# A two-block transformer kernel: high parts of the weights by converting DMA, six slots, first inputs reordered

## The reference

```
proj = nx @ w_in;  h = h + mixed @ w_out
h = h + square(relu(nm @ w_ff1)) @ w_ff2
... second layer: w_in_2, w_branch, w_out_2 ...
h = h + (silu(nm @ w_ffn_gate) * (nm @ w_ffn_up)) @ w_ffn_down
```

## Time and profile before

| | us |
|---|---|
| median of 3 runs | 1414.1 (1411.76 to 1415.14) |
| the profiled execution | 1414.06 |
| its span in the trace | 1412.4 |
| PE busy in it | 1386.7 (98%) |
| ScalarE busy | 865.4 (61%) |
| VectorE busy | 624.8 (44%) |
| POOL busy | 192.7 (14%) |

### The profile page before, as it was taken

How to read it: one execution, slowest core, us unless ns; L and a number is a source line. 1 busy time by engine, 2 the same in 40 slices (tenths; PEclk the granted TensorE clock), 3 DMA queues, 4 the chain that set the end, 5 groups by cost and what they waited for, 6 DMA issues and landing times.

```text
span 1412.4 us, 17525 instructions
## 1 busy us (share of the span) xinstructions
PE 1386.7 (98%) x6784; PEld 1119.7 (79%) x6784; DVE 624.8 (44%) x1216; ACT 865.4 (61%) x1272; POOL 192.7 (14%) x227
## 2 busy tenths in 40 slices
PE   9999999999999999999989999999999999999999
PEld 6977966788888888887867768787788888888887
DVE  6055365521211212357578779954534422341232
ACT  5574566654544535666678778776557645663561
POOL 0210000111111111111100001011111111111110
PEclk9999999999999999999999999999999999999999
DMA  7975544698888888877745556679988888888975
GB/s 227 248 167 131 143 117 97 151 208 194 189 196 196 194 189 199 189 166 170 169 100 119 120 119 163 169 172 269 221 198 186 192 192 200 192 192 194 197 164 125
DMA packets 72791, 248.00 MB, mean 176 GB/s; under 512 B 8098, under 2 KB 8114, under 8 KB 72580
## 3 DMA queue, kind: packets, MB, share of 16 engines
q0 software_dynamic: 31536, 113.54, 47.0%
q1 hardware_dynamic: 40452, 131.73, 28.9%
q10 hardware_dynamic: 720, 1.61, 0.3%
HBM read 240.52 MB, written 6.32 MB: 175 GB/s over the span
## 4 chain that ended last, share of the span: by engine, by line
PE 78%; ACT 8%; DVE 8%; issue 3%; DMA 2%; SPq 0%; DVEq 0%; ACTq 0%
PE bank L466 24%; PE bank L470 24%; PE bank L473 24%; ACT WH L770 2%; ACT WL L778 1%; PE bank L581 1%; PE bank L600 1%; DVE eb L1416 1%; DMA RAW<-in_w_out 1%; PE bank L624 1%; PE bank L614 1%; ACT eb L924 1%; ACT hs L720 1%; DMA gates<-hs 1%; DVE eb L1412 0%
## 5 line engine op out<-in xcount | busy, mean ns | idle before, releaser
L466 PE MATMUL bank<-NH,WH 128*128 128x512 f32 x1152 | 466.4, 406 | 3.5 <-ACT NH L875 1.7
L470 PE MATMUL bank<-NL,WH 128*128 128x512 f32 x1152 | 449.2, 391 | 1.0 <-DVE NL L1160 0.5
L473 PE MATMUL bank<-NH,WL 128*128 128x512 f32 x1152 | 449.3, 391 | 0.0
L770 ACT ACTIVATE WH<-RAW 128x1024 fp32r<-128x1024 f32 (+2 forms) x227 | 235.2, 1037 | 204.8 <-PE bank L473 191.5
L466 PEld LDWEIGHTS bank<-NH,WH 128*128 128x128 f32 x1152 | 216.9, 188 | 69.0 <-issue 26.3
L470 PEld LDWEIGHTS bank<-NL,WH 128*128 128x128 f32 x1152 | 217.0, 188 | 47.8 <-issue 3.8
L473 PEld LDWEIGHTS bank<-NH,WL 128*128 128x128 f32 x1152 | 216.8, 188 | 46.2
L778 ACT ACTIVATE WL<-WH 128x1024 fp32r<-128x1024 f32 (+2 forms) x219 | 229.5, 1048 | 5.6
L470 PE MATMUL bank<-AL,WH 128*128 128x512 f32 x432 | 168.2, 389 | 0.0
L466 PE MATMUL bank<-AH,WH 128*128 128x512 f32 x432 | 168.1, 389 | 0.0
L473 PE MATMUL bank<-AH,WL 128*128 128x512 f32 x432 | 168.0, 389 | 0.0
(11 more groups left out here) (288 smaller groups left out, 1637.7 us busy)
## 6 DMA issues: line engine op xcount, KB each, us to landing
RAW<-in_w_in SPq DMA_DIRECT2D x64, 512.0 KB, 5.5
RAW<-in_w_ff SPq DMA_DIRECT2D x64, 512.0 KB, 6.2
WL<-in_w_ff POOLq DMA_DIRECT2D x64, 512.0 KB, 8.7
WL<-in_w_in POOLq DMA_DIRECT2D x62, 512.0 KB, 7.8
RAW<-in_w_gu SPq DMA_DIRECT2D x44, 512.0 KB, 6.6
WL<-in_w_gu POOLq DMA_DIRECT2D x44, 512.0 KB, 8.8
RAW<-in_w_down SPq DMA_DIRECT2D x20, 512.0 KB, 5.1
WL<-in_w_down POOLq DMA_DIRECT2D x20, 512.0 KB, 8.7
```

The source lines that it names most:

```text
L466: e.matmul(o, a[0], a[1], start=(k == 0), stop=False)
L470: e.matmul(o, b[0], b[1], start=False, stop=False)
L473: mm = e.matmul(o, c[0], c[1], start=False, stop=(k == t.kt - 1))
L770: e.activation(WH[p % HL][:, 0:n], RAW[p % RAWS][:, 0:n], ACT.Copy).then_inc(*act.sig("high", p))
```

## The change

It does these things:

- From the tenth piece on (`ADDED` = 9), the high part no longer comes over RAW and a ScalarE copy. POOL issues a DMA from the fp32 weights straight into WH, whose type is fp32r, so the transfer converts (`highs`). It is issued at `split_time(p)`, after the product that last used the slot. The negation stands 8.5 after it, the accumulating transfer for WL 10 after it.
- `HL` is 6 instead of 5. RAW moves to memory that the gates' temporaries use later.
- The first unit is cut into pieces of 1, 1, 2, 2, 2 blocks (128 KB each for the first two), so there are 228 pieces.
- The first four blocks of x come in halves of 64 partitions: the lower over SP, the upper over ScalarE's queue.
- VectorE makes NH and NL of block 0 before the low part of the first piece. PE runs two more matmuls of 128 columns on zeros.

```diff
-HL = 5
+HL = 6
...
-            n = 2 if u == 0 else n
-            for k in range(0, kt, n):
-                self.pieces.append((u, k, min(n, kt - k)))
+            at = [0, 1, 2, 4, 6, 8] if u == 0 else [*range(0, kt, n), kt]
+            self.pieces += [(u, a, b - a) for a, b in zip(at, at[1:])]
...
-        RAW = [sb(f"RAW{i}", PIECE) for i in range(RAWS)]
...
+        RAW = [sb(f"RAW{i}", PIECE) for i in range(RAWS)]
+        top[0] = temps
         gx_, gb_, gt_ = two("gX", 5), two("gB", 4), two("gT")
...
-        ADDED = 8
+        ADDED, NEGATED = 9, 8.5
...
+        def high(p):
+            return ("high" if p < ADDED else f"high_loaded{p % HL}", p)
...
-            if p < 5:
-                return [-20.0, -18.4, -15.4, -13.4, -11.5][p]
-            return plan.used[p - HL] + 0.1
+            if p < HL:
+                return [-20.0, -18.4, -17.4, -15.4, -13.4, -11.5][p]
+            return (4.1, 8.1, 12.1)[p - HL] if p < ADDED else plan.used[p - HL] + 0.1
 
         def low_time(p):
-            return split_time(p) + (3.0 if p >= ADDED else 0.05)
+            return split_time(p) + (NEGATED + 1.5 if p >= ADDED else 0.05)
...
-                for n in (S, S, UC):
+                for n in (S, S, UC, P, P):
...
-                        pe.wait_ge(("high", p), hi(x, k0 + k))
+                        pe.wait_ge(high(p), hi(x, k0 + k))
...
-                e.dma_start(first_in, A["xT"][:, 0:64 + S]).then_inc(*act.sig("x0", by=16))
-                at["gains",] = at["x0",]
-                for i in range(2, 8, 2):
+                e.dma_start(first_in[64:P, :], A["xT"][64:P, 0:64 + S]).then_inc(*act.sig("x_upper0", by=16))
+                for i in range(1, 4):
+                    e.dma_start(hT[64:P, i, :], x_src[64:P, i, :]).then_inc(*act.sig(f"x_upper{i}", by=16))
+                for i in range(4, 8, 2):
                     e.dma_start(hT[:, i, :], x_src[:, i, :]).then_inc(*act.sig(f"x{i}", by=16))
...
             def splits():
-                for p, (u, k, m) in enumerate(plan.pieces):
+                for p, (u, k, m) in enumerate(plan.pieces[:ADDED]):
...
                     if p >= ADDED:
-                        yield split_time(p) + 1.5
+                        yield split_time(p) + NEGATED
...
-                yield -19.0
-                dve.wait_ge(("x0",))
+                yield -20.5
+                dve.wait_ge(*x_in(0))
...
-                    yield -18.9 + k
-                    row("attn", "n_attn", k, g_attn, [(f"x{k}",), ("gains",)])
+                    yield -18.9 + k if k else -20.4
+                    row("attn", "n_attn", k, g_attn, x_in(k))
...
+            def highs():
+                for p, (u, k, m) in enumerate(plan.pieces):
+                    if p < ADDED:
+                        continue
+                    yield split_time(p)
+                    st, name, i, kt, cols, k0 = plan.units[u]
+                    src = A[name] if i is None else A[name][i]
+                    u0, j0, m0 = plan.pieces[p - HL]
+                    pool.wait_ge(("product", "block", u0, j0 + m0 - 1))
+                    e.dma_start(WH[p % HL][:, 0:m * cols], src[:, k * cols:(k + m) * cols]).then_inc(
+                        *pool.sig(f"high_loaded{p % HL}", p, by=16))
...
-            yield from merge(zeros(), lows(), masks())
+            yield from merge(zeros(), highs(), lows(), masks())
...
-                for p, (u, k, m) in enumerate(plan.pieces):
+                for p, (u, k, m) in enumerate(plan.pieces[:ADDED]):
                     yield -29.0 + 2 * p if p < RAWS else split_time(p - RAWS) + 0.1
...
-                for i in range(1, 8, 2):
-                    yield -28.5 + i
+                yield -28.0
+                e.dma_start(first_in[0:64, :], A["xT"][0:64, 0:64 + S]).then_inc(*sp.sig("x_lower0", by=16))
+                for i in (1, 2, 3):
+                    yield (-26.0, -24.0, -23.5)[i - 1]
+                    e.dma_start(hT[0:64, i, :], x_src[0:64, i, :]).then_inc(*sp.sig(f"x_lower{i}", by=16))
+                for i in (5, 7):
+                    yield -23.0
                     e.dma_start(hT[:, i, :], x_src[:, i, :]).then_inc(*sp.sig(f"x{i}", by=16))
```

More of the change, by code:

```diff
@@ L333, in build_program, with x_in @@
                 operands[st] = (NH, NL, "n_attn" if st in ("qG", "kG", "vG", "gG", "qD", "kD", "vD") else "n_second")
+        def x_in(k):
+            return [(f"x_lower{k}",), (f"x_upper{k}",)] if k < 4 else [(f"x{k}",)]
         on_act = {"vG", "vD", "vS", "vH"}
-        ADDED = 8
+        ADDED, NEGATED = 9, 8.5
         def freed(t):
@@ L749, in prologue @@
                         e.dma_start(cf, A["c_f32"]).then_inc(*act.sig("const", by=16))
-                    act.wait_ge((f"x{k}",), ("gains",))
+                    act.wait_ge(*x_in(0), *x_in(k))
                     e.activation(NH[:, k, :], hT[:, k, :], ACT.Copy, scale=g_attn[:, k:k + 1]).then_inc(*act.sig(*hi("n_attn", k)))
@@ L754, in prologue @@
                     square("attn", k, acc if k == 0 else sq[k % 2], 1.0,
-                           [(f"x{k}",)] + ([("square_sum", "attn", k - 2)] if k > 2 else []))
+                           x_in(k) + ([("square_sum", "attn", k - 2)] if k > 2 else []))
             def square(ph, k, to, scale, waits):
@@ L774, in negated @@
                     if p >= ADDED:
-                        yield split_time(p) + 1.5
+                        yield split_time(p) + NEGATED
                         n = m * plan.units[u][4]
-                        act.wait_ge(("high", p))
+                        act.wait_ge(high(p))
                         e.activation(WL[p % HL][:, 0:n], WH[p % HL][:, 0:n].bitcast(F32), ACT.Copy,
@@ L826, in gla @@
                 yield gla_time(c, 0) + 0.1
-                act.wait_ge(("gla_gate", c), ("gains",))
+                act.wait_ge(("gla_gate", c), *x_in(0))
                 if c:
@@ L1462, in gain_product @@
                 yield plan.start(("f2", 3))
-                dve.wait_ge(("gains",), lo(("f1", 0), 0))
+                dve.wait_ge(*x_in(0), lo(("f1", 0), 0))
                 e.tensor_tensor(g_fn, g_fin, g_n1, ALU.mult).then_inc(*dve.sig("gain_product"))
@@ L1469, in lower_bound @@
                 yield plan.start("qS") + 1.0
-                dve.wait_ge(("gains",))
+                dve.wait_ge(*x_in(0))
                 e.tensor_tensor(m_, la, lb2, ALU.max).then_inc(*dve.sig("lb", 0))
@@ L1715, in vector @@
             streams += [mixed_split("mixed", k, T_A1 - 2.0 + 0.2 * k, []) for k in range(4)]
-            streams += [dilated(), to_h("wo0", "wo0", lambda k: (f"x{k}",))]
+            streams += [dilated(), to_h("wo0", "wo0", lambda k: x_in(k)[-1])]
             streams += [mixed_split("mixed", k, plan.start("wo1") - 0.6 + 0.1 * k, []) for k in range(4, 8)]
@@ L1783, in weights @@
                     if p >= RAWS:
-                        sp.wait_ge(low(p - RAWS) if p - RAWS < ADDED else ("high", p - RAWS))
+                        sp.wait_ge(low(p - RAWS))
                     e.dma_start(RAW[p % RAWS][:, 0:m * cols], src[:, k * cols:(k + m) * cols]).then_inc(
```

## The result

The changed kernel takes 1493.95 us (median of 4 runs, 1489.64 to 1496.07) against 1414.62 of the kernel before in the same session: ratio 1.0559, 95% interval 1.053 to 1.0589. It is slower by 79 us, and outside the forecast range of 1394 to 1413.

The account below looks back on a forecast made before the run. PE itself was taken as the bound, except in stick-breaking attention, where ScalarE's queue and VectorE's scans bound. 7.0 + 2.9 + 2.0 + 0.8 + 0.4 + 0.7 - 0.8 = 13.0 us off 1414.1 gave 1401 us, range 1394 to 1413.

Parts of the forecast that it names:

- POOL: POOL's queue: 219 more issues of 0.86 us, 193 us busy becoming 382; nothing queued behind held up, cost 0.
- the last rival: POOL's in-order wait could keep the six slots from being filled ahead; given no chance of its own.
- Its second sign of being wrong: In the profile after: ScalarE's negation waiting on its DMA more than some 50 us in all, PE waits behind it.
- The latency: WH landing before ScalarE's negation: 6.1 to 8.8 us against 5.8 allowed; cost 0, bound 3 us per stage change.
- The price of the conversion: DMA engines in dense stages: converting costs like plain (30%), both kinds stay at 87%, cost 0 under PE's cover.
- The slower rival: 270 to 600 and 965 to 1412 us: converting costs like accumulating, 114% wanted, about 1510 us; chance 0.10.
- 700 to 825 us: Stick-breaking attention: removing ScalarE's WH copies shortens PE's waits, 7.0 us gained.
- no low clock near 725 us: 723.3 to 729.1 us: with a shorter wait no fall to half clock; half of 5.8, 2.9 us gained.
- 172 to 270 us: PE idle 3.4 us, one to two copies ahead of each wait; 2.0 us gained (0 to 3.4).
- 825 to 965 us: PE idle 6.9 us, but its two largest kinds of wait are for VectorE; 0.8 us gained.
- The -0.8 for the two early pieces: Twelfth and fourteenth pieces have only 22 units (15 us) from release to use; 0.8 us lost, bounds 0 and -4.
- The start: First unit: VectorE's order and shorter first copy give 0.4, fewer bytes 0.3; 0.7 us gained, bounds -1.0 and 2.5.

Follow-up runs that it names:

- the version with both places later: Kernel after with ScalarE's negation 16.5 instead of 8.5 and the accumulating issue 18 instead of 10 units behind the release, from the 17th piece: 1400.22 us, ratio 0.9908.
- the 1398.39 us version: Kernel after with negation at 16.5 and accumulating issue at 18 units, and the start of the kernel before: 1398.39 us, ratio 0.989.

## Why the prediction was wrong

**The step that failed** is the one under *POOL*: "What is queued behind its new wait (for the product six pieces back) is the next WL issue, due 6 to 10 units after; in PE's order that product is always earlier ... Nothing: 0." It looked at what stands behind the new wait and not at what the new issue itself stands behind: the WL issue waits for the negation of a transfer that was issued just before it. The same hole is in the last rival: "By the order above no wait reaches past a release; I give it no chance of its own." That rival is what happened: in the kernel after POOL stood 1006 us for negations, and a pair of pieces took 12.0 us where PE wants 10.9. Late landings stood in the forecast with a chance of 0.03 only. Its second sign of being wrong came true: ScalarE waited 481 us for WH at its negations, where some 50 was the limit named.

**The latency** was bounded by RAW's 6.1 and WL's 8.8 us, with both ends named. The landing was 9.4 in the loop, past the upper end, where each pair of highs goes into the one software queue right behind two accumulating transfers; with one low between two highs it was 6.2 to 7.0. The bound of 3 us for each of some ten changes of stage was too small for two reasons: ScalarE stood up to 10.6 us at the first MLP's weights, and the long stalls brought stretches at half clock, which the prediction counted as a gain at 725 us and nowhere as a loss. The path of 15.6 us against 24.5 was right for one piece and missed that the issue of a pair waited for the pair before it: at two pieces a turn the turn has to be shorter than 10.9 us, and it was 12.0.

**The price of the conversion** was right within 9%: 87% forecast, 88.7 measured, 174 ns a packet against 159. The slower rival I named (DMA engines full, 1510) ended near the measured time for a cause that the trace does not show: share 76.5%, and the loss went without a byte less being moved. That its number is near is luck.

**The gains** were right in kind and nearly in size, as the version with both places later shows against the earlier trace rows: 700 to 825 us 8.2 missing became 1.8 (7.0 forecast, 6.4 measured); no low clock near 725 us (2.9 forecast); 172 to 270 us 3.4 became 1.1 (2.0 forecast, 2.4 measured); 825 to 965 us 6.9 became 4.6 (0.8 forecast, 2.2 measured). The stages of that version start 1 us later than before at 184 us, 2.5 earlier at 704 and 13 earlier at 838. With the last window moved by 13 us, 4.1 are missing instead of 4.6, so the readings hold. From the first wT matmul of the stick-breaking stage to the last, 116.9 us became 107.5: 9.4, where 7.0 + 2.9 was forecast. That version's 13.2 us below the kernel before of its session stand beside the 13.0 of the sum; that the two agree so closely is partly luck, since the sum did not have the loss of the start (below), and the three windows without the clock gave 11.0 us where 9.8 was forecast. And it is not the kernel for which the forecast was made. The -0.8 for the two early pieces does not show: in that version, as in the kernel before, PE is busy 37.00 of 37.00 us from 23 to 60 us and 111.35 of 112.00 from there to 172.

**The start** was mis-sized and had the wrong sign: +0.7 forecast, -3.1 measured on the kernel before, -1.8 on the later version, beyond the lower bound of -1.0 (the -1.8 is within the noise of its two runs). The bytes argument counted what was ahead of the second block and not of the third, whose lower half stands sixth on SP's queue. The rule of the Trainium skill that the prediction cites against the halves ("Trainium Kernel Development and Optimization", Key Constraints: transfers from several queues run on the same 16 engines and interleave) agrees with the sign: -3.1 us.

**One row was misread.** The longest accumulating issue of the kernel before (1.55 us) was taken as a sign that VectorE holds GpSimd up. The trace shows it at 52.8 us, right behind three copies of masks by POOL itself (the last of them 1.89 us from 51.32), while VectorE did nothing until 53.4. So the row shows POOL's own work ahead of the issue, not VectorE. The sum did not use it.

## What to carry to other kernels

Where an in-order queue issues both a transfer and a later one that depends on it through another engine, write out who stands behind whom: the order of the issues bounds how many transfers are in flight, and a chain that is short enough for one piece can still be too long for the pace. A place in the order can act as a step and not a slope (4.6 us from 10 to 11 units, 81 from 11 to 13), so try the places on both sides of every crossing. And count a stall at PE with the clock stretch that follows it.

## What the runs showed of the hardware

- A transfer that converts fp32 to fp32r costs the DMA engines nearly what a plain one costs: 174 ns against 159 for a packet of 4096 bytes, where an accumulating one takes 327 (88.7% against 87.0% for both kinds together).
- A converting issue that stood alone in POOL's queue took 0.55 us in the 1400.22 us version, an accumulating one 0.86 in the kernel before (medians from 300 to 600 us). Where one issue directly followed another, both kinds took 0.88 to 0.90.
- With VectorE making the negation, POOL's accumulating issues for the MLP's weights took 1.00 us on average instead of 0.88. The trace shows which ones: from 300 to 600 us the 23 issues during which a negation of VectorE ran took 1.04 to 1.19 us, and the 27 others 0.86 to 0.90, though during 24 of them another instruction of VectorE ran. The Trainium skill ("DMA: Bandwidth & Descriptors", SWDGE vs HWDGE vs iDMA) says that VectorE, in its 2-port mode, locks GpSimd out of the memory where it writes descriptors; this agrees for the negation. The trace does not name the mode, but the negation passes 1024 columns in 0.73 us, where VectorE's subtraction for AL takes 0.69 for 512.
- PE's stalls of 3.5 and 6.5 us were followed by 5 to 7 us at half clock. A wait of 1.8 us for wT in the 1400.22 us version was not (1.00 from 700 to 760 us), an equal one in the 1398.39 us version was (0.97 in that window). So the length of the stall alone does not decide, and the prediction's argument from the sum of several waits was weak.
